# Fourteen half products instead of sixteen in four slabs of a projection

## The reference

```
h = rmsnorm(x, mix_norm[0])                       # 256 x 1024
proj = h @ w_in                                   # 1024 x 2304
qa, ka, va, qb, kb, vb = split(proj)              # 8 heads dilated, 8 heads banded with 2 key heads
qa, ka, qb, kb = rmsnorm per head of 64
x = x + concat(attention_a, attention_b) @ w_out
```

## Time and profile before

| | us |
|---|---|
| median of 3 runs | 622.19 (621.80 to 622.41) |
| the profiled execution | 622.04 |
| its span, first to last instruction | 620.0 |
| PE busy in the span | 570.4 |
| DVE, ACT, POOL busy | 182.9, 136.0, 9.1 |
| weights and inputs moved | 233.35 MB, 376 GB/s on average |

### The profile page before, as it was taken

The page is one execution under the profiler, slowest core; times in us unless marked ns, Lnnn a source line. Parts: engine busy times, 40 slices in busy tenths (PEclk is TensorE's granted clock), DMA queues, the critical chain, the costliest instruction groups (busy, mean ns, idle before and its releaser), DMA issues.

```text
span 620.0 us, 9561 instructions
## 1 busy us (share of the span) xinstructions
PE 570.4 (92%) x3900; PEld 377.2 (61%) x3900; DVE 182.9 (30%) x591; ACT 136.0 (22%) x351; POOL 9.1 (1%) x25
## 2 busy tenths in 40 slices
PE   8999999998999969979999999999899996998897
PEld 7888876793554354344468876779355435345454
DVE  3334355253120110111036586415312010111101
ACT  3143546340011101101031357524001110100101
POOL 1100000000000000000002000000000000000000
PEclk9999999999999989998999999999999997999799
DMA  8999947498999999999999995529899999999996
GB/s 325 423 422 421 420 167 238 157 372 360 427 427 442 418 436 436 423 428 419 421 414 421 423 419 232 205 100 368 346 428 429 438 422 432 432 430 424 420 421 269
DMA packets 24242, 233.35 MB, mean 376 GB/s; under 512 B 2688, under 2 KB 3328, under 8 KB 6656
## 3 DMA queue, kind: packets, MB, share of 16 engines
q1 hardware_dynamic: 22176, 227.14, 88.2%
q10 hardware_dynamic: 2016, 5.52, 2.5%
HBM read 231.60 MB, written 1.05 MB: 375 GB/s over the span
## 4 chain that ended last, share of the span: by engine, by line
PE 70%; DMA 21%; issue 3%; DVE 3%; ACT 2%; ACTq 0%; DVEq 0%
DMA ring<-in_moe_w 20%; PE banks L813 15%; PE banks L1033 13%; PE banks L899 8%; PE banks L1007 7%; PE banks L1103 6%; PE banks L1119 5%; PE banks L859 2%; PE banks L788 2%; PE banks L887 2%; PE banks L876 2%; PE banks L1018 1%; PE banks L910 1%; PE banks L935 1%; DMA gains_xT<-in_xT 1%
## 5 line engine op out<-in xcount | busy, mean ns | idle before, releaser
L1033 PE MATMUL banks<-ring,desk 128*32 128x512 f32 x736 | 89.0, 624 | 9.2 <-DMA ring<-in_moe_w 9.1
L813 PE MATMUL banks<-ring,hT 128*128 128x256 f32 x416 | 94.6, 382 | 0.0
L813 PEld LDWEIGHTS banks<-ring,hT 128*128 128x128 f32 x416 | 77.3, 190 | 13.2 <-issue 3.6
L1328 ACT ACTIVATE desk<-banks 128x256 f32<-128x256 f32 x16 | 6.1, 383 | 273.6 <-PE banks L1033 273.6
L899 PE MATMUL banks<-heads,ring 128*128 128x256 f32 x256 | 61.9, 387 | 0.1
L1033 PEld LDWEIGHTS banks<-ring,desk 128*32 128x32 f32 x736 | 23.2, 114 | 60.7 <-issue 55.7
L1007 PE MATMUL banks<-desk,hT 128*128 128x128 f32 x384 | 49.3, 291 | 10.6 <-issue 10.6
L1007 PEld LDWEIGHTS banks<-desk,hT 128*128 128x128 f32 x384 | 48.9, 207 | 11.9 <-issue 11.4
L899 PEld LDWEIGHTS banks<-heads,ring 128*128 128x128 f32 x256 | 46.4, 190 | 12.6 <-issue 6.9
L1103 PE MATMUL banks<-ring,desk 128*32 128x512 f32 x400 | 46.2, 595 | 6.7 <-ACT desk L1330 5.7
L1119 PE MATMUL banks<-desk 128*128 128x256 f32 x224 | 52.1, 386 | 0.0
(11 more groups left out here) (180 smaller groups left out, 584.1 us busy)
## 6 DMA issues: line engine op xcount, KB each, us to landing
ring<-in_moe_w SPq DMA_DIRECT2D x66, 1024.0 KB, 27.1
ring<-in_moe_w SPq DMA_DIRECT2D x16, 4096.0 KB, 28.0
ring<-in_moe_w SPq DMA_DIRECT2D x17, 2048.0 KB, 11.6
ring<-in_ab_w_in SPq DMA_DIRECT2D x8, 1024.0 KB, 16.9
shared<-in_moe_w SPq DMA_DIRECT2D x8, 1024.0 KB, 7.1
shared<-in_moe_w SPq DMA_DIRECT2D x2, 4096.0 KB, 32.2
shared<-in_moe_w SPq DMA_DIRECT2D x3, 2048.0 KB, 13.0
ring<-in_c_w_in SPq DMA_DIRECT2D x5, 1024.0 KB, 20.3
```

The costliest lines, as they stand in the source:

```text
L813: ins = pe.matmul(bank2(SLAB_BANK[layer][s], NT)[:, t, :], hT[:, c, t * P:(t + 1) * P], w[:, c, :], start=(c == 0 and t == 0), stop=(c == ...
L1033: ins = pe.matmul(bank(0)[j * SLOTS:(j + 1) * SLOTS, :], gathered_of(rd, place)[:, c, j * SLOTS:(j + 1) * SLOTS], w[:, j, :], start=(c == ...
```

## The change

Slabs 3 and 4, and slabs 6 and 7, are multiplied as pairs. The product of the 256x1024 tokens by the 1024x512 of two slabs is cut into 2x2 blocks, tokens by halves of the tokens (rows) and of the inputs, weights by halves of the inputs and by slab. Strassen's scheme in Winograd's form computes the four tiles by seven products of 128x512 by 512x256 instead of eight; each product is four matmuls, as a part is. The sums of operands that it needs are made on GpSimd in SBUF: four of the tokens once (128x512 each, after the input is normalised) and four of the weights for each pair (128x1024 each, when both slabs have landed; for the second pair also when the first is done). They lie in three slots of the ring (16 to 18), which the loads therefore get only after slab 7; units 16 to 18 go to the slots of slabs 0 to 2 and so on.

The sums of results: products 2 and 3 are added in PSUM, ScalarE copies the first product, the fifth and the first tile, VectorE makes the others (four additions of 128x256 a pair, and one more of that size in SBUF). ScalarE squares the finished slabs from SBUF. In `ORDER_0` the products take the places of the parts; part 0 of slab 5 and of slab 8 now stand a step earlier or later. `halves` is replaced by tiles where the rotation tables lie later, and all engines' loops call the new functions at ("product", pair, j). The diff, cut to its core:

```diff
+PAIRED = ((3, 4), (6, 7))
+SUMS_AT = 16
...
-    free = {s: (-1, None) for s in range(LOW)}
+    last = PAIRED[-1][1]
+    free = {s: (-1, None) if s < SUMS_AT else (last, last) for s in range(LOW)}
...
-        halves = shared[:, 3840:4096].rearrange("p (t n) -> p t n", t=NT)
...
+        sums_of = ring[:, SUMS_AT * UNIT:LOW * UNIT]
+        token_sum = sums_of[:, 0:UNIT].rearrange("p (i c t) -> p i c t", i=4, c=NC // 2)
+        weight_sum = sums_of[:, UNIT:UNIT + 3 * D].rearrange("p (i c n) -> p i c n", i=3, c=NC // 2)
+        late_tiles = shared[:, 7168:7168 + 512].rearrange("p (t n) -> p t n", t=NT)
+        kept, widened = late_tiles[:, 0, :], late_tiles[:, 1, :]
+        fifth = shared[:, 7680:7680 + 256]
...
-            + each("turn", 0) + parts(3, 0) + each("turn", 1) + parts(3, 1)
-            + each("scores", 0) + parts(3, 2, 3) + each("normalise", 0) + parts(4, 0, 1)
-            + each("turn_prob", 0) + each("scores", 1) + parts(4, 2, 3) + each("prob_values", 0) + each("normalise", 1)
-            + parts(5, 0, 1) + each("norm", 1)
-            + each("turn_prob", 1) + parts(5, 2, 3) + each("turn", 3) + parts(6, 0) + each("turn", 4) + parts(6, 1)
-            + each("scores", 2) + each("prob_values", 1) + each("normalise", 2) + parts(6, 2, 3) + parts(7, 0)
-            + each("turn_prob", 2) + each("scores", 3) + parts(7, 1) + each("prob_values", 2)
-            + each("normalise", 3) + parts(7, 2, 3) + each("residual", 0) + each("norm", 2)
-            + each("turn_prob", 3) + parts(8, 0, 1) + each("prob_values", 3) + parts(8, 2, 3) + each("norm", 3)
+            + each("turn", 0) + products(0, 1) + each("turn", 1) + products(0, 5)
+            + each("scores", 0) + products(0, 6, 7) + each("normalise", 0) + products(0, 2, 3)
+            + each("turn_prob", 0) + each("scores", 1) + products(0, 4) + parts(5, 0)
+            + each("prob_values", 0) + each("normalise", 1) + parts(5, 1) + each("norm", 1) + parts(5, 2)
+            + each("turn_prob", 1) + parts(5, 3) + each("turn", 3) + products(1, 1) + each("turn", 4) + products(1, 5)
+            + each("scores", 2) + each("prob_values", 1) + products(1, 6, 7) + each("normalise", 2) + products(1, 2)
+            + each("turn_prob", 2) + each("scores", 3) + products(1, 3) + each("prob_values", 2)
+            + products(1, 4) + each("normalise", 3) + parts(8, 0) + each("residual", 0) + each("norm", 2)
+            + each("turn_prob", 3) + parts(8, 1, 2) + each("prob_values", 3) + parts(8, 3) + each("norm", 3)
...
-                return halves
+                return late_tiles[:, :, 0:2 * HD]
...
+            def add_tokens():
+                a11, a21 = hT[:, 0:NC // 2, 0:P], hT[:, 0:NC // 2, P:SEQ]
+                a12, a22 = hT[:, NC // 2:NC, 0:P], hT[:, NC // 2:NC, P:SEQ]
+                s1, s2, s3, s4 = [token_sum[:, i, :, :] for i in range(4)]
+                pool.wait_ge(s_h, 4)
+                for i, (out, a, b, op) in enumerate(((s1, a21, a22, ALU.add), (s2, s1, a11, ALU.subtract),
+                                                     (s3, a11, a21, ALU.subtract), (s4, a12, s2, ALU.subtract))):
+                    after(pool, s_tsum, i)
+                    G.tensor_tensor(out, a, b, op).then_inc(s_tsum, 1)
+
+            def add_weights(pair):
+                wa, wb = [ring_of(s).rearrange("p (c n) -> p c n", c=NC) for s in PAIRED[pair]]
+                b11, b21, b12, b22 = wa[:, 0:4, :], wa[:, 4:8, :], wb[:, 0:4, :], wb[:, 4:8, :]
+                t2, t3, t4 = [weight_sum[:, i, :, :] for i in range(3)]
+                for s in PAIRED[pair]:
+                    unit_arrived(pool, s)
+                if pair:
+                    pair_done(pool, pair - 1)
+                for i, (out, a, b) in enumerate(((t3, b22, b12), (b12, b12, b11), (t2, b22, b12), (t4, b21, t2))):
+                    after(pool, s_wsum, 4 * pair + i)
+                    G.tensor_tensor(out, a, b, ALU.subtract).then_inc(s_wsum, 1)
+
+            add_tokens()
+            add_weights(0)
...
+            add_weights(1)
...
-                    if b in SLAB_BANK[layer][:s]:
+                    pair = [i for i, (first, _) in enumerate(PAIRED) if layer == 0 and b in SLAB_BANK[0][first:s]]
+                    if pair:
+                        pe.wait_ge(s_c11, pair[-1] + 1)
+                    elif b in SLAB_BANK[layer][:s]:
...
+            def product(pair, j):
+                first, second = PAIRED[pair]
+                x, y = pair_banks(pair)
+                wa, wb = slab_weights(0, first), slab_weights(0, second)
+                low_half, high_half = slice(0, NC // 2), slice(NC // 2, NC)
+                rows_0, rows_1 = slice(0, P), slice(P, SEQ)
+                def multiply(out, a, b, start=False):
+                    for c in range(NC // 2):
+                        ins = pe.matmul(out, a[:, c, :], b[:, c, :], start=(start and c == 0), stop=(c == NC // 2 - 1),
+                                        skip_group_check=True)
+                    return ins
+                if j == 1:
+                    if pair:
+                        slab_taken(pe, 0, PAIRED[pair - 1][1])
+                    else:
+                        slab_taken(pe, 0, 0)
+                    slab_arrived(0, first)
+                    multiply(x[:, 0, :], hT[:, low_half, rows_0], wa[:, low_half, :], start=True).then_inc(s_prod, 1)
+                elif j == 5:
+                    slab_taken(pe, 0, first - 1 if pair else 1)
+                    pe.wait_ge(s_tsum, 1)
+                    pe.wait_ge(s_wsum, 4 * pair + 2)
+                    multiply(y[:, 0, :], token_sum[:, 0, :, :], wb[:, low_half, :], start=True).then_inc(s_prod, 1)
+                elif j == 6:
+                    pe.wait_ge(s_p1, pair + 1)
+                    pe.wait_ge(s_tsum, 2)
+                    pe.wait_ge(s_wsum, 4 * pair + 3)
+                    multiply(x[:, 1, :], token_sum[:, 1, :, :], weight_sum[:, 0, :, :]).then_inc(s_prod, 1)
+                elif j == 7:
+                    pe.wait_ge(s_p5, pair + 1)
+                    pe.wait_ge(s_tsum, 3)
+                    multiply(y[:, 1, :], token_sum[:, 2, :, :], weight_sum[:, 1, :, :]).then_inc(s_prod, 1)
+                elif j == 2:
+                    pe.wait_ge(s_u, pair + 1)
+                    multiply(x[:, 0, :], hT[:, high_half, rows_0], wa[:, high_half, :]).then_inc(s_prod, 1)
+                elif j == 3:
+                    pe.wait_ge(s_v, pair + 1)
+                    pe.wait_ge(s_tsum, 4)
+                    slab_arrived(0, second)
+                    multiply(y[:, 0, :], token_sum[:, 3, :, :], wb[:, high_half, :]).then_inc(s_prod, 1)
+                else:
+                    pe.wait_ge(s_wsum, 4 * pair + 4)
+                    multiply(y[:, 1, :], hT[:, high_half, rows_1], weight_sum[:, 2, :, :]).then_inc(s_used, 2)
...
+            def room_for(s):
+                i = norm_slabs_before(0, s)
+                act.wait_ge(s_slab, i - 1)
+                act.wait_ge(s_hT_ps, turns_before(*NORMED[i - 1]))
+            def take_product(pair, j):
+                first, second = PAIRED[pair]
+                x, y = pair_banks(pair)
+                if j == 1:
+                    product_done(act, pair, 1)
+                    A.activation(kept, x[:, 0, :], ACT.Copy).then_inc(s_p1, 1)
+                elif j == 5:
+                    product_done(act, pair, 5)
+                    A.activation(fifth, y[:, 0, :], ACT.Copy).then_inc(s_p5, 1)
+                elif j == 2:
+                    product_done(act, pair, 2)
+                    room_for(first)
+                    A.activation(unnormed(0, first)[:, 0, :], x[:, 0, :], ACT.Copy).then_inc(s_c11, 1)
+                elif j == 4:
+                    act.wait_ge(s_c11, pair + 1)
+                    for k, s in enumerate((first, second)):
+                        kind = SLAB_PLAN[0][s][0]
+                        i = norm_slabs_before(0, s)
+                        w = 2 * HD if kind == "shared2" else 4 * HD
+                        act.wait_ge(s_tiles, 3 * pair + 2 + k)
+                        if kind == "shared2":
+                            act.wait_ge(s_rstd, 1)
+                            for t in range(NT):
+                                ins = A.activation(values[0][:, t, 512:512 + 2 * HD], late_tiles[:, t, 2 * HD:4 * HD],
+                                                   ACT.Copy, scale=rstd[:, t:t + 1])
+                            ins.then_inc(s_val, 1)
+                        act.wait_ge(s_slab, i - 1)
+                        A.activation(square[:, i % 2, 0:NT * w].rearrange("p (t n) -> p t n", t=NT), unnormed(0, s),
+                                     ACT.Square).then_inc(s_sqh, 1)
...
+            def add_product(pair, j):
+                first, second = PAIRED[pair]
+                x, y = pair_banks(pair)
+                if j == 6:
+                    product_done(dve, pair, 6)
+                    dve.wait_ge(s_p1, pair + 1)
```

(57 more changed lines are left out.)

## The result

The changed kernel takes 632.92 us, median of 6 runs (631.98 to 633.21), against 621.91 (621.50 to 622.41) for the kernel before on the same chip: a ratio of 1.0174 [1.0161, 1.0187], 11.0 us slower. A second comparison on another occasion gave 632.82 and 1.0172 [1.0154, 1.0189]. The forecast was 630.0, +8.0.

What follows compares the result with a forecast made beforehand. TensorE's matmuls bound the mixer, whose end sets the later weight transfer, so mixer time carries one for one: -3.46 + 5.0 + 1.9 + 3.6 + 0.9 = +7.9 on 622.04, 630.0 us. Range 624.1 to 634; 8 in 10: 619.2 to 635.

Steps and rivals of the forecast that it cites:

- the sums do not hide: Rival, before turn 0: VectorE's small operations do not wait for GpSimd's whole instruction, norm on time, 619.5 us; chance 0.18.
- the price is not 3.65: Rival, GpSimd's subtractions: 3.56 ns a column is real work, turn 0 12 and turn 3 11 late, 645 us; chance 0.09.
- the mixer's shift reaches the end: Against the rival of no net change, 622 us: more operations pass each gap, or the weight transfer absorbs the shift; chance 0.08.
- Removed: TensorE, both pairs: seven products replace eight parts, twice, taking 2 x 1.73 = 3.46 us off.
- Price: GpSimd: one 128x1024 weight subtraction costs 2.2 us with start and gap; bounds 2.1 and 3.65.
- Turn 0 idle: First pair: GpSimd's subtractions hold VectorE's norm of slabs 0 and 1, so TensorE idles 5.0 us before turn 0.
- Clock: TensorE behind the idle before turn 0: lower granted clock adds 1.9 us; bounds 0 and 2.9.
- Second pair: GpSimd's second four subtractions delay VectorE's normalising of probabilities 1 and norm of slabs 3 and 4: 3.6 us.
- Order of the queue: VectorE, second pair: additions after products 7 and 4 stand ahead of normalising, making turn_prob 2 and 3 late, 0.9 us together.
- Loads: Units 16 to 18 lose their own slots and loads 22 to 26 wait for the second pair; gaps in transfers hide this.
- token sums: GpSimd, 13.7 to 18.5 us: four sums of 512 columns run while VectorE has 5.04 us of idle; nothing is lost.

Runs made afterwards that it cites:

- the last VectorE version: Changed kernel with all sums on VectorE instead of GpSimd and normalise moved ahead of products 7 and 4 in the second pair: 618.07 us, ratio 0.9935.
- the trace with fills: Kernel before with the changed slots and GpSimd's sums read by no product, its eight weight subtractions replaced by fills with zero: 621.07 us, one run.
- the filler: Changed kernel with 24 matmuls of the identity on TensorE ahead of turn 0: 630.63 us.
- the order experiment: Changed kernel with normalise ahead of product 7, and of product 4, in the second pair: 631.65 us.
- quarters: Changed kernel with each GpSimd weight subtraction cut into four of 128x256: 623.26 us, ratio 1.0016.
- the kernel with the sums alone: Kernel before with the changed plan of slots and all sums made on GpSimd but read by no product: 632.71 us, ratio 1.0189.

## Why the prediction was right, and where its sizes were off

The direction, the range and the mechanism held: a lock for whole instructions, read from one stretched L1467 and two router multiplications. Its rivals fell: the sums do not hide (turn 0 waits 5.61 for VectorE), the price is not 3.65, and the mixer's shift reaches the end (11.1 at turn 6, 10.7 at the end). By term:

- **Removed, 3.46.** Right; the last VectorE version gets 3.46 from slab 1 to turn 6.
- **Price, 2.2 a subtraction: 2.36**, 2.42 with the gap. I divided two short stretches (0.53), which I had inferred from the ends of four operations, by their columns. Alone the 128x288 multiplication takes 0.67 (two in 1.29 in the trace with fills), and the subtraction measures 2.13 ns a column, not 1.85.
- **Turn 0 idle, 5.0: 5.83 late.** Of the ten small operations six were through by 29.5 and the seventh by 31.7, much as "four to six by 30.6" had it. That two pass per gap, given as the better case, was the rule, and the price was higher than I had it. These two errors offset each other; that 5.0 came near is in part luck.
- **Clock, 1.9: 2.18**; the filler gave back 2.19 at the same place.
- **Second pair, 3.6: 5.61. This is the mis-sized step**, 2.0 of the 3.1 us by which my sum of +7.9 was low; turn 0 makes 0.8 and the clock 0.3. "I take the middle" stood between L1543 passing freely and being held. It is held, 2.41 us in the median. So turn_prob 1, not the norm, is late, and the norm's small operations come after the subtractions, unhindered. TensorE waits 3.28, then 0.56, and runs slowly between (1.11 for records that take 0.60, and 2.86 for 1.89, together 1.5). The 4.2 to 5.5 that I gave for "held" would have been near in size, though not in kind: the idle is 3.84 in all, and the 1.5 of clock I had not put into this term. (By its own numbers the 9.1 in my working should be 9.2, which moves the term by 0.1 at most.) The Trainium skill (SBUF — State Buffer, the list of practical consequences) lets a tensor_scalar in its two-port mode take the shared ports; by the 3.83 and 4.74 of the L1719 rows, the trace agrees.
- **Order of the queue, 0.9: 0.91.** Right, and taken back by the order experiment in its trace. Why the second half is late is as I argued: the additions stand ahead of the normalising.
- **Loads, 0; token sums, 0.** Right. The token sums did hold small operations of VectorE (0.16 became up to 1.13 us), but the delay went into the idle time that I had named: 5.04 before, 2.04 after.
- **The range.** Its upper end, 634, takes 6.0 for turn 0, a figure that no line of my working gives. The measured 5.83 lies just under it.

The sum of the measured terms, -3.46 + 5.83 + 2.18 + 5.61 + 0.91 = +11.1, agrees with the +11.0 of the medians.

## What to carry to other kernels

Work moved to an idle engine is free only if it shares nothing with an engine on the path: look in the trace for an operation of usual length that is stretched while the other engine runs, and cost the move by held operations, not by busy time. Where it must be there, cut it short: quarters took back 9.7 of 11 us, although they made GpSimd's own work some 40% longer. And ask first whether the busier engine has a hole for it: VectorE did the same sums in half the time and made the loss of 11 us a gain of 4.

## What the runs showed of the hardware

- **A one-input instruction of GpSimd holds VectorE's two-input operations only near its start.** A multiplication of 128x1024 takes 2.8 us; what met its start was free after 0.8 to 0.9 us, and what came later passed. A subtraction of 2.36 us held them to its end.
- **A fill (0.95 us) holds tensor_scalars of VectorE and no operation with two inputs**, by 0.76 at most.
- **GpSimd is held too.** Beside VectorE's own weight sums, in the kernel with these and the order, its two 128x288 multiplications took 1.75 and 1.65 us instead of 0.67.
- **Splitting costs GpSimd some 40%**: 0.86 us for each 128x256 (13.76 / 16), so 3.44 where one instruction of four times the size takes 2.42.
- **The clock does not follow from the length of an idle alone.** After idles of 5.61 and 5.84 the turn took 1.12 instead of 0.60. After 2.40 it also ran slow (1.05, then 3.22 for a product of 1.89), and so it did after 3.28. After 3.37, in the kernel with the sums alone, it did not (0.65, then 1.89), nor after the same 3.28 in the run with the order changed (0.66, then 1.89). TensorE had been busy without a break before both the 2.40 and the 3.37. What parts them is left open; a short idle of TensorE is to be costed with and without some 1.8 us of clock.
